# Half passes of a projection moved from the second-to-last pair and head into the last ones, with the gate taken by halves and the finished rows split later

## The reference, cut to what matters

```python
# fox: one pair of heads at a time
proj = h @ w_in                  # q, k, v, z
s = q @ k.T * scale + c[t] - c[s]        # c: running sum of log f
pr = softmax(causal(s));  o = pr @ v
return (o * silu(z)) @ w_out

# dil: one head at a time, three groups (128,1), (512,4), (2048,16)
proj = h @ w_in                  # q, k, v for each group, one z
o_g, lse_g = window_attention(q_g, k_g, v_g)
o = sum(softmax(lse)_g * o_g)
return (o * silu(z)) @ w_out
```

## Time and profile before

| | |
|---|---|
| median of 3 runs | 2908.32 us (2904.5 to 2914.92) |
| profiled execution, first to last instruction (span) | 2902.8 us; no other time of it is listed |
| PE busy | 2792.1 us, 96% of the span |
| PEld, DVE, ACT, POOL busy | 75%, 41%, 31%, 35% |
| mean granted TensorE clock | 0.980 |

### The profile page before, as it was taken

The page is one execution under the profiler, slowest core; times in us unless marked ns, Lnnn a source line. Parts: engine busy times, 40 slices in busy tenths (PEclk is TensorE's granted clock), DMA queues, the critical chain, the costliest instruction groups (busy, mean ns, idle before and its releaser), DMA issues.

```text
span 2902.8 us, 41142 instructions
## 1 busy us (share of the span) xinstructions
PE 2792.1 (96%) x16908; PEld 2166.9 (75%) x16908; DVE 1184.7 (41%) x2813; ACT 902.8 (31%) x1701; POOL 1022.5 (35%) x447
## 2 busy tenths in 40 slices
PE   7999998899999999998999999999999999999998
PEld 5766675567777777776887878888888888887887
DVE  6989997556433333335335011111112121114323
ACT  5322413552333343344123122222222222224112
POOL 2542481133322222223632433333333333333531
PEclk8999998999999999999999999999999999999999
DMA  4110121121211111112121111111111111113211
GB/s 114 39 30 22 30 69 51 48 91 38 67 51 38 38 50 52 52 44 95 58 79 53 56 39 37 50 39 44 37 51 45 37 44 44 44 42 141 66 51 65
DMA packets 221334, 155.56 MB, mean 54 GB/s; under 512 B 25254, under 2 KB 207948, under 8 KB 221020
## 3 DMA queue, kind: packets, MB, share of 16 engines
q1 hardware_dynamic: 210076, 122.55, 14.6%
q10 hardware_dynamic: 11072, 30.39, 3.0%
HBM read 133.45 MB, written 19.47 MB: 53 GB/s over the span
## 4 chain that ended last, share of the span: by engine, by line
PE 51%; DVE 2%; issue 1%; ACT 1%; DMA 0%; ACTq 0%; DVEq 0%
PE proj L904 14%; PE proj L906 14%; PE proj L905 14%; PE out L1423 2%; PE score L1371 1%; PE score L1401 1%; PE score L1380 1%; PE proj L944 1%; PE out L905 0%; PE out L906 0%; PE out L904 0%; PE out L1390 0%; DMA y_scratch<-arena 0%; DVE arena L2343 0%; DVE arena L2470 0%
## 5 line engine op out<-in xcount | busy, mean ns | idle before, releaser
L904 PE MATMUL proj<-act_hi,w_hi 128*128 128x512 f32 x2560 | 1033.7, 404 | 10.4 <-ACT hT L1846 4.4
L906 PE MATMUL proj<-act_hi,w_lo 128*128 128x512 f32 x2560 | 1005.8, 393 | 0.0
L905 PE MATMUL proj<-act_lo,w_hi 128*128 128x512 f32 x2560 | 1005.3, 393 | 0.0
L777 POOL TENSOR_TENSOR w_hi<-w_raw,ones 128x1024 fp32r<-128x1024 f32 x175 | 420.6, 2403 | 1598.6 <-PE proj L906 1596.4
L904 PEld LDWEIGHTS proj<-act_hi,w_hi 128*128 128x128 f32 x2560 | 486.3, 190 | 122.8 <-issue 17.2
L906 PEld LDWEIGHTS proj<-act_hi,w_lo 128*128 128x128 f32 x2560 | 485.3, 190 | 104.7
L905 PEld LDWEIGHTS proj<-act_lo,w_hi 128*128 128x128 f32 x2560 | 486.6, 190 | 95.8 <-issue 0.2
L779 POOL TENSOR_TENSOR w_lo<-w_raw,w_hi 128x1024 fp32r<-128x1024 f32 x175 | 432.2, 2470 | 13.7
L1846 ACT ACTIVATE arena<-proj 128x512 f32<-128x512 f32 x236 | 175.9, 754 | 669.5 <-PE proj L906 645.5
L2470 DVE SCALAR_TENSOR_TENSOR arena<-arena,score 128x256 f32<-128x256 f32 (+1 forms) x192 | 76.1, 427 | 717.7 <-PE score L1371 676.9
L1872 ACT ACTIVATE arena<-score 128x512 f32<-128x512 f32 (+3 forms) x264 | 115.7, 486 | 197.9 <-PE score L1232 197.4
(11 more groups left out here) (268 smaller groups left out, 2874.1 us busy)
## 6 DMA issues: line engine op xcount, KB each, us to landing
w_raw<-dil_w_in_dram SPq DMA_DIRECT2D x80, 512.0 KB, 3.7
w_raw<-fox_w_in_dram SPq DMA_DIRECT2D x32, 512.0 KB, 4.1
w_raw<-w_in_dram SPq DMA_DIRECT2D x23, 512.0 KB, 3.8
y_scratch<-arena ACTq DMA_DIRECT2D x21, 512.0 KB, 3.6
act_lo<-y_scratch SPq DMA_DIRECT2D x21, 512.0 KB, 6.2
arena<-decay_scratch ACTq DMA_DIRECT2D x16, 512.0 KB, 5.9
w_raw<-ple_w_gate_dram SPq DMA_DIRECT2D x16, 512.0 KB, 3.7
arena<-x_dram SPq DMA_DIRECT2D x12, 512.0 KB, 5.0
```

Of the source, the lines that this page charges most:

```text
L777: pool.tensor_tensor(hi, raw, one.unsqueeze(1).broadcast_to([P, KB, P]), ALU.mult).then_inc(w_hi_done, 1)
L904: pe.matmul(bank, hi, a_hi, start=first, stop=False)
L905: pe.matmul(bank, hi, a_lo, start=False, stop=False)
L906: return pe.matmul(bank, lo, a_hi, start=False, stop=last)
```

## The change

1. *Fox pair 6* (`pair_units`, p == 6) deals out only five half passes of pair 7, (0,0), (0,1), (1,0), (1,1), (2,0), as ten parts: one part in each of tiles 0 to 5, two in tiles 6 and 7.
2. *Fox pair 7* does its other five units itself: X (3,0) and T (4,0) between its first two scores, T (2,1) after them, X (3,1) after the transposes of tile 0, T (4,1) at the end of tile 0.
3. *Dil head 6* deals out 20 units in place of 24. *Dil head 7* does T (11,0) ahead of the turns of head 6's last two tiles, T (9,1) after `scores(1)`, X (12,0) and X (10,1) in tile 0, T (11,1) at the end of tile 0, X (12,1) in tile 1. (12,0) and (12,1) were there before.
4. The gate's tanh on ACT and product on DVE are done by halves of 512 tokens in the last pair and head; the products stand in tiles 0 and 3.
5. Rows are split later: fox row 0 in tile 4, 1 and 2 in tile 5, 3 to 6 in tile 6; dil 0 and 1 in tile 4, 2 and 3 in tile 5, 4 to 6 in tile 6. `out_rows` of dil uses row 0 in tile 5, 1 and 2 in tile 6, 3 to 6 in tile 7.

```diff
-LATE_ROWS = {3: (0,), 4: (1,), 5: (2,), 6: (3,), 7: (4, 5, 6)}
+LATE_ROWS = {5: (0,), 6: (1, 2), 7: (3, 4, 5, 6)}
 SPLIT_AT = {1: (0, 1), 2: (2,), 3: (3,), 4: (4,), 5: (5,), 6: (6,)}
...
+LATE_UNITS = dict(fox=((3, 0), (4, 0), (2, 1), (3, 1), (4, 1)),
+                  dil=((11, 0), (12, 0), (9, 1), (10, 1), (11, 1), (12, 1)))
+FOX_PARTS = ((0, 1), (1, 2), (2, 3), (3, 4), (4, 5), (5, 6), (6, 8), (8, 10))
+SPLIT_LATE = dict(dsa=SPLIT_AT, fox={4: (0,), 5: (1, 2), 6: (3, 4, 5, 6)}, dil={4: (0, 1), 5: (2, 3), 6: (4, 5, 6)})
...
+    if last_head:      # proj_units, for dil head 6
+        every = [(h // 2, h % 2, None) for h in range(halves) if (h // 2, h % 2) not in LATE_UNITS[kind]]
+        units = every[len(every) * t // NT:len(every) * (t + 1) // NT]
...
+    if kind == "fox" and p == PASSES["fox"] - 2:      # pair_units
+        parts = [unit(n // 2, n % 2) for n in range(*FOX_PARTS[t])]
+        return [], parts[0], (parts[1] if len(parts) > 1 else None), []
...
+                    late = kind == "fox" and not follow      # PE, pair
                     for half in range(2):
-                        pe.wait_ge(pass_free[half], p * NB + (first + NB))
+                        pe.wait_ge(pass_free[half], p * NB + first + ((3, 2)[half] if late else NB))
                     scores(0, 0)
+                    if late:
+                        project(p, [(3, 0, None)])
+                        spread(NT - 1, p - 1)
+                        project(p, [(4, 0, None)])
...
                     scores(1, 0)
+                    if late:
+                        project(p, [(2, 1, None)])
...
+                        elif late and i == 0:
+                            project(p, [(3, 1, None)])
...
                         scores(i + 2, 0)
+                        if late and i == 0:
+                            project(p, [(4, 1, None)])
...
-                        project(p, [(NB - 1, 0, None)])      # PE, head
+                        project(p, [(NB - 1, 0, None) if follow else (11, 0, None)])
                         turn(N - 2, p - 1)
                         turn(N - 1, p - 1)
                     scores(1, 0)
                     if p > 0:
-                        project(p, [(NB - 1, 1, None)])
+                        project(p, [(NB - 1, 1, None) if follow else (9, 1, None)])
...
+                        elif t == 0:
+                            project(p, [(12, 0, None), (10, 1, None)])
+                        elif t == 1:
+                            project(p, [(12, 1, None)])
                         elif t in LATE_ROWS:
                             out_rows(m, LATE_ROWS[t])
...
+                        if t == 0 and not follow:
+                            project(p, [(11, 1, None)])
...
-                for j in SPLIT_AT.get(i, ()):      # ACT, split_rows
+                for j in SPLIT_LATE[("dsa", "fox", "dil")[m]].get(i, ()):
...
+                def late_gate(Q, half):
+                    tok = slice(half * 512, half * 512 + 512)
+                    act.wait_ge(pass_free[half], (PASSES[kind] - 1) * NB + base + (5 if kind == "fox" else 12))
+                    act.activation(R["e"][:, tok], Q["g"][:, tok], ACT.Tanh, scale=0.5).then_inc(late_tanh, 1)
...
+                    if late:      # ACT, fox pair 7
+                        projected(p, own, [(3, 0, None), (4, 0, None)])
+                        late_gate(Q, 0)
+                        projected(p, own, [(2, 1, None)])
```

More of the change, by code:

```diff
@@ L562, in build @@
                          "ms root rstd on ot gate y ysent pool pmm py z neg")
+        late_tanh, late_gated = GL["diff"], GL["pool"]
+        LATE_BEFORE = dict(fox=2, dil=4)
         PLE = dict(sems("ple", "in tr ev ph pl up t h"), before={})
@@ L1305, in one @@
                                 residual_turn(t)
+                        if late and i in (0, 4):
+                            pe.wait_ge(pass_free[i // 4], p * NB + first + 4)
                         values(i, 0)
                         values(i, 1)
+                        if late and i == 2:
+                            pe.wait_ge(pass_free[1], p * NB + first + 2)
                         scores(i + 2, 0)
+                        if late and i == 0:
+                            project(p, [(4, 1, None)])
                         if follow:
@@ L1430, in one @@
                     for half in range(2):
-                        pe.wait_ge(pass_free[half], p * NB + first + NB - (1 if p > 0 else 0))
+                        pe.wait_ge(pass_free[half], p * NB + first + (NB if p == 0 else NB - 1 if follow else (11, 9)[half]))
                     for piece in range(pieces):
@@ L1466, in one @@
                         if t == 0 and p > 0:
-                            for half in range(2):
+                            for half in range(2 if follow else 1):
                                 pe.wait_ge(pass_free[half], p * NB + first + NB)
+                        if t == 4 and not follow:
+                            pe.wait_ge(pass_free[1], p * NB + first + NB)
                         for c in range(0 if len(chunks[t]) <= 2 else 2, 4):
@@ L1886, in pair @@
                         store(p - 1)
-                    for half in range(2):
-                        act.wait_ge(pass_free[half], p * NB + (base + NB))
-                    if follow:
-                        decay(p + 1, 1 - turn_)
-                    act.activation(R["e"], Q["g"], ACT.Tanh, scale=0.5).then_inc(S["gate"], 1)
+                    late, own = kind == "fox" and not follow, set_of(kind, p)
+                    if late:
+                        projected(p, own, [(3, 0, None), (4, 0, None)])
+                        late_gate(Q, 0)
+                        projected(p, own, [(2, 1, None)])
+                    else:
+                        for half in range(2):
+                            act.wait_ge(pass_free[half], p * NB + (base + NB))
+                        if follow:
+                            decay(p + 1, 1 - turn_)
+                        act.activation(R["e"], Q["g"], ACT.Tanh, scale=0.5).then_inc(S["gate"], 1)
                     for i in range(NT):
@@ L1894, in pair @@
                         turned(i, 0)
+                        if late and i == 0:
+                            projected(p, own, [(3, 1, None)])
                         if follow:
@@ L1902, in pair @@
                             exp(i + 1)
+                        if late and i == 0:
+                            projected(p, own, [(4, 1, None)])
+                            late_gate(Q, 1)
                         if follow:
@@ L1951, in one @@
                             exp(t + 1)
+                        if t == 0 and not follow:
+                            projected(p, turn_, [(11, 1, None)])
+                            late_gate(Q, 1)
                         if follow:
@@ L2428, in one @@
                             reciprocals(t)
-                        if t == 0:
+                        if kind == "fox" and not follow:
+                            if t in (0, 3):
+                                gated_half(kind, R, Q, t // 3)
+                        elif t == 0:
                             wait_pass(dve, S["gate"], before + p, 2, 1)
```

37 lines of the change are left out of this document (25 added, 12 removed).

## The result

The changed kernel takes **2925.53 us** in the median of six runs (2922.24 to 2928.04), the kernel before 2905.97 in six runs beside them. The ratio is 1.0062, 95% interval 1.0052 to 1.0073: slower by 19.6 us, where +12.9 was forecast. The profiled execution spans 2924.5 us, 21.7 more than the one of before.

The account below looks back on a forecast made before the run. PE is busy nearly everywhere, so time is PE's work plus its holes plus low clock. Fox +8.0, dil +3.9 and DVE against POOL +1.0 give +12.9, on the median of 2908.3 us 2921; range 2906 to 2928.

Parts of the forecast that it names:

- Part A: Fox pair 6, tile 0: uncovered hole grows to 3.5 us, +2.7, and a clock fall behind it, +3.3.
- Part B, the head: Head of fox pair 7: holes of 3.55 and 0.45 us close, full clock returns, less two eviction waits; −4.0 us.
- Part B, tiles 1 and 2: Fox pair 7, tiles 1 and 2: DVE sets the pace, so full clock gives back little; −0.5 us.
- Part C: Late fox rows: loads hidden, second copy in tile 5 +0.7 us, tile 7 waits at POOL's pace +5.8 us.
- Part D: Dil head 6, tile 7 and next scores: waits of 0.7, 0.8 and 0.8 us on ACT and evictions; +2.3 us.
- Part E: Dil head 7: waits at the head go, −3.2 us; tiles 3 and 4 lose a row of cover each, +1.6.
- Part F: Dil tile 7: rows 4 to 6 are copied behind exp(7) and split at POOL's pace; +3.2 us.
- Part G: DVE against POOL in tiles 4 to 6: one of 16 subtractions was long, most pass unharmed; +1.0 us.
- strict rival: DVE is stopped by POOL each time and the clock falls again in fox's row wait; 2926 us, chance 0.17.
- No dip: Fox pair 6's hole opens but the clock stays up; sum +9.6 us or less, 2914 at low ends, chance 0.28.
- The lead holds: Tile 0's cover keeps DVE and ACT ahead through tile 7, no row is waited for; 2899 us, chance 0.08.
- The bounds: Lower and upper limits of all terms over both layers together, put at +2 to +27 us.

Follow-up runs that it names:

- e6: Changed kernel, but fox pair 6 deals out two parts in tile 0 and one in tile 6; 2922.81 us, 1.0058 of the kernel before.
- e1: Kernel before with only the fox part of the change and its late fox rows, dil restored; 2920.85 us, 1.0052 of the kernel before.
- e7: Changed kernel, but in fox pair 7 ACT evicts X (3,0) ahead of the store of pair 6; 2919.99 us, 1.0054 of the kernel before.
- e10: e9 plus T (2,1) ahead of T (4,0) in fox pair 7 and ACT's half tanh later; 2902.53 us, 0.9986 of the kernel before.
- e3: Kernel before with only the change's late row splits and uses, no projection moved; 2917.18 us, 1.0043 of the kernel before.
- e8: Changed kernel, but in dil head 6's last tile X (8,1) and T (9,0) stand ahead of values; 2920.46 us, 1.0049 of the kernel before.
- e12: e10 with DVE's subtraction for dil's last row reading PSUM and placed earlier (low part wrong thereby); 2900.82 us, 0.9983 of the kernel before.
- e9: Changed kernel with fox and dil rows split two per tile from tile 3, plus e6, e7 and e8; 2905.28 us, 0.9998 of the kernel before.
- e11: e10's fox code with the dil code of the kernel before; 2903.32 us, 0.9992 of the kernel before.
- e5: Changed kernel, but dil's rows are split two per tile from tile 3; 2921.22 us, 1.0050 of the kernel before.

## Why the prediction was right or wrong

The direction was right, the time lay in the range, and the two largest terms, pair 6 and tile 7 of fox, were right in kind. The sum, +12.9, is 6.8 short of the 19.7 of the two sections: terms that were too small miss by some 11 and terms that were too large by some 4. That 2921 us stands only 4.5 under the measured 2925.5 is in part luck, since the median of before came out 2.3 lower in the later runs (2905.97 for 2908.32).

| step | forecast | measured | from |
|---|---|---|---|
| A fox pair 6 | +6.0 | +5.0 | hole 0.81 → 3.54, fall 1.7, a new hole of 0.54 in tile 4 |
| B head of pair 7 | −4.0 | −0.3 | 1238.08 → 1321.85 became 1240.56 → 1329.01, +4.7 less pair 6's 5.0 |
| B tiles 1, 2 | −0.5 | −2.15 | 9.23 → 7.08 |
| C tiles 3 to 6 | +0.7 | +0.3 | 23.39 → 23.66 |
| C tile 7 | +5.8 | +8.6 | 14.15 → 22.74 |
| D dil head 6 | +2.3 | +4.1 | what is left of dil's +8.3 |
| E, F head 7 | +1.6 | +4.2 | 43.55 → 64.59, less 16.8 of moved work |
| G | +1.0 | about +0.7 | hole of 0.68 behind a held subtraction, in tile 2 of head 7 (counted in the row above) |

(Fox tiles are cut at the first transposes of tiles 1 and 3 and at `out_first`; head 7 runs from its first scores, 2650.92 and 2651.50, to D1; the moved work is three times 5.44 and an X half.)

**Part A** was right: a hole of 3.5 forecast, 3.54 measured, and a fall of the clock behind it (e6 shows both go with the cover). The 3.3 taken for the fall was twice what this trace shows; e1, with the same code there, shows 3.0.

**Part B, the head, failed.** It closed the hole of 3.55 as it said, but counted ACT's new work at 1.0 us and didn't walk ACT's list in order. The store of pair 6 stands ahead of the first eviction, and what it needs is the end of the chain that Part A had described for pair 6. PE reaches the same bank first: 2.15, a fall of 1.5, and 0.47 at X (3,1). e7 shows that the store's place is a part; in e10, where T (2,1) on the other bank stands between X and T (4,0), the rest is gone too.

**Part B, tiles 1 and 2** were mis-sized by 1.65 us for a false reason, that DVE sets the pace there. With PE at full clock they took 7.08 us in place of 9.23, although their two holes, 1.35 and 0.53, both behind ACT, are larger than the 1.15 of before; so most of the difference was PE's own time at low clock.

**Part C**: tile 7 was right in mechanism, and this is the main term: row 6 is used 10.58 us after the start of ACT's first copy (1359.08 → 1369.66), forecast 10.6. Too small was the price of the clock: a term of 1.7 at most was given to it, and 4.4 were lost here; the transposes, `out_first(1)` and values then ran at 1.2 GHz. The same four waits lost 1.6 in e1 and 2.4 in e3. The loads were hidden, as said.

**Part D** had the three holes to 0.1 to 0.2 us each (0.47, 1.13, 0.69 for 0.7, 0.8, 0.8); the term lacked the fall of the clock, 1.7, which e8 removes together with the first two.

**Part E** was right in what goes (−3.1) and in what opens in tiles 2 and 3 (0.68 + 0.87 for 1.6). The missed term is row 0: the prediction counted the cover that leaves tiles 3 and 4, and not that rows 0 and 1 are copied behind exp(5) and row 0 is used a tile later, when exp(5) + 1.04 + 2.4 us isn't over. 2.16 and a fall of 1.6; e3 has the same hole with no unit moved.

**Part F**: measured +1.9 of +3.2. The rows start at 2704.80 and values at 2712.45: 7.65 us, before 4.39, and 1.36 of the difference is the row more. The end came 9.8 us after exp(7), as forecast; but PE reached the rows 2.2 us after exp(7) and not 0.8, since tile 6 has two rows.

**Part G and the strict rival.** The size is about right, the reading wrong. "One of 16" took the largest value of the group for the only long one. The rows of that group in before hold three, 1.96 at 584.88, 2.25 at 1325.99 and 1.80 at 1355.67, and the same subtraction in dil (L2518) has three more, of 0.80, 1.98 and 1.55. One of them:

```profile
1355.67 1.80 DVE L2413 TENSOR_TENSOR act_lo<-arena,act_hi 128x128 fp32r<-128x128 f32 x1
```

All six began beside an instruction of POOL and ended 0.1 to 0.2 us behind it, and the others, of 0.29, began with POOL idle. It is the rule in all fourteen traces, from 1225 to 1400 and from 2620 to 2730 us, for two kinds of instruction: copies from SBUF to SBUF (0.07 to 0.1 us behind POOL's end) and additions and subtractions of 128x128 with two SBUF inputs (0.1 to 0.2). It isn't the rule for everything that reads SBUF alone: reciprocals and the reductions of the scores kept their time, this one of after beside POOL's row of 2690.72 among them:

```profile
2691.61 0.95 DVE L2552 TENSOR_REDUCE arena<-arena 128x1 f32<-128x768 f32 x1
```

The Trainium skill (Advanced Engine Details and Errata, GPSIMD Details) says that the Pool engine conflicts with DVE instructions "in a 2-port perf mode or with two SBUF inputs"; the traces agree for two SBUF inputs, with one POOL instruction's remainder (at most 2.48 us in all, at 1313.01 in e10) as the price, and e12 shows that one PSUM input ends it. Where PE doesn't wait for what is behind it, it costs nothing: in fox tile 7 of after a subtraction of 1.80 us stands beside POOL's rows and no wait is behind it. Both conditions of the strict rival came true, the holds and a further fall of the clock in the row wait, and its 2926 us is nearer to the measured 2925.5 than the forecast. Its sum was near partly by luck: the holds cost about 0.7 us in place of the 4 that it had for them, and the head of pair 7, which it shares with the forecast, was missed by 3.7.

**The other rivals.** "No dip" falls: beside the norm's, five falls of the clock stand in the two sections of after, one in those of before. "The lead holds" was right in one point only, that the cover at the head gives the full clock back; exp(7) was never ahead, and even e10 is 3 us faster, not 9. The bounds, put at +2 to +27, add up to +1.2 and +27.7; nothing hangs on it.

## What to carry to other kernels

When filler work is moved from one stage to the next, walk the lists of the engines that must drain it in their own order, and look at which bank comes twice in a row: a hole closed on PE reopens where an eviction queues behind something that ends late. Work that is delayed "until just before it is used" needs the producers' pace counted from the last event that lets them start: four rows at 2.36 us behind the last exp cost 8.6 us with the clock behind them, and spread over earlier tiles 1.4. Before GpSimd work is packed beside VectorE's, look for VectorE copies from SBUF, and sums of two SBUF inputs, on the way to PE, and give them a PSUM input where the sum allows it. On this kernel a wait of PE of 2 us or more, or several close together, is to be priced with the clock behind it: 0 to 4.4 us on top. Cutting one long wait into short ones can gain by the clock alone, as in e9 and e10. Holes of 1.46 and 1.47 us in dil had a fall of 1.7 behind them in e1, e9 and e11, and those of 1.45 in e5 and e10 had none.

## What the runs showed of the hardware

A DVE copy from SBUF, or an addition or subtraction of two SBUF inputs, that starts while POOL executes one of its own doesn't slow down in proportion, but ends just behind it: 0.29 us became 1.08, 1.25, 1.80, 2.15 and 2.32, by where in POOL's 2.36 us it started. DVE gets in between two POOL instructions, so the hold is never longer than one of them. DVE instructions with a PSUM input beside them kept their time (0.29 in e12; 0.28 for L2478 in after, beside POOL's row of 1360.20), and so did reductions (0.69 for 128x512, 0.95 for 128x768) and reciprocals (0.15, 0.16) that read SBUF alone.

The same hole doesn't cost the same clock. The one of pair 6, left as it is in after, e1 and e7, lost 1.7, 3.0 and 2.9 us of full speed, and its twin of 3.55 in before's pair 7 4.2; the one of 2.15 at T (4,0) lost 1.5 in after and nothing in e6; a fall near 720 us, in a block that no edit touches, lost 1.5 in some kernels and 4.9 in others. Four waits of 0.6 to 1.4 us, 2.3 us apart, lost 4.4 in after, though none of them is over 1.4, and 1.6 and 2.4 in e1 and e3. Where the falls are the same the sections repeat closely: after's fox code took 141.93, 141.91 and 141.86 us in after, e5 and e8. The runs of one kernel spread with the clock too: among those of before, six with a mean granted clock of 0.983 average 2902.6 us and eight with 0.979 average 2908.3. So a difference of 2 to 5 us between two single executions can be the clock's alone; a median needs several runs, and a section has to be read with its falls beside it.
